# 128 bytes more between the high and the low weight buffer of a float32 transformer kernel

## What is computed

```python
h = rms_norm(x, pre_mix_norm);  p = h @ w_in            # then four mixers -> y
x = x + rms_norm(y @ w_out, post_mix_norm)
x = x + rms_norm(conv_ffn(rms_norm(x), ffn_up, ..., ffn_down), post_ffn_norm)
# second block
x = x + 0.5 * swiglu(rms_norm(x), ffn1_w_gate, ffn1_w_up, ffn1_w_down)
proj = rms_norm(x) @ w_in_2                             # then two kinds of attention
y = sigmoid(g_dil) * (o_dil @ w_dil_branch) + sigmoid(g_diff) * (o_diff @ w_diff_branch)
x = x + y @ w_out_2
x = x + 0.5 * swiglu(rms_norm(x), ffn2_w_gate, ffn2_w_up, ffn2_w_down)
```

## The kernel before, in words

| moving rows | high rows | low rows |
|---|---|---|
| moving, gated, gated_branch, branch | 192 | 192 |
| mixed (`w_out` alone) | 0 | 0 |

## Time and profile before

### The profile page before, as it was taken

One profiled execution on the slowest core, in us unless ns is written; L12 is line 12 of the kernel. 1 busy time (PEld: TensorE's weight loads), 2 busy tenths in 40 slices (PEclk: granted clock), 3 DMA queues, 4 the chain that ended last, 5 costly groups with the idle time before them and its releaser, 6 DMA issues.

```text
span 3354.0 us, 59341 instructions
## 1 busy us (share of the span) xinstructions
PE 3336.8 (99%) x19746; PEld 2930.5 (87%) x19746; DVE 2238.2 (67%) x2874; ACT 1745.4 (52%) x2588; POOL 533.8 (16%) x502
## 2 busy tenths in 40 slices
PE   9999999999999999999999999999999999999999
PEld 8888888888888888888888888888888888888888
DVE  7878587777744565655555699766687655655544
ACT  5455565555544554544444555554565554544443
POOL 0215111111100011111100066511100111111000
PEclk9999999999999999999999999999999999999999
DMA  6535555555566555555566655545556555555665
GB/s 214 163 114 157 183 171 190 189 189 191 187 193 189 179 180 194 188 188 192 188 190 191 215 175 175 190 156 160 172 192 199 192 188 192 189 188 191 186 194 174
DMA packets 176036, 616.21 MB, mean 184 GB/s; under 512 B 20912, under 2 KB 21584, under 8 KB 175568
## 3 DMA queue, kind: packets, MB, share of 16 engines
q1 hardware_dynamic: 175520, 609.84, 57.0%
q10 hardware_dynamic: 432, 5.24, 0.4%
HBM read 610.81 MB, written 4.19 MB: 183 GB/s over the span
## 4 chain that ended last, share of the span: by engine, by line
PE 94%; DVE 3%; issue 1%; ACT 1%; DMA 1%; POOL 0%; DVEq 0%; SPq 0%; ACTq 0%; POOLq 0%
PE acc L462 59%; PE acc L465 30%; DVE weights_low L312 1%; PE ps_wide L391 1%; PE acc L477 1%; ACT weights_high L305 0%; PE ps_narrow L2551 0%; PE ps_wide L2527 0%; PE acc L480 0%; DVE halves_memory L567 0%; PE ps_scale L2932 0%; DMA weights_raw<-in_w_in 0%; DMA weights_raw<-in_w_diff_branch 0%; DVE halves_memory L3010 0%; ACT arena L801 0%
## 5 line engine op out<-in xcount | busy, mean ns | idle before, releaser
L462 PE MATMUL acc<-moving_halves,weights_high 128*128 128x512 f32 x6304 | 1971.2, 394 | 1.9 <-DVE x_T L2820 1.9
L312 DVE TENSOR_TENSOR weights_low<-weights_raw,weights_high 128x1024 fp32r<-128x1024 f32 (+1 forms) x1172 | 1431.2, 1235 | 716.7 <-ACT weights_high L305 715.7
L305 ACT ACTIVATE weights_high<-weights_raw 128x1024 fp32r<-128x1024 f32 (+1 forms) x1172 | 1207.8, 1032 | 768.7 <-PE acc L465 741.9
L465 PEld LDWEIGHTS acc<-moving_halves,weights_low 128*128 128x128 f32 x6304 | 1183.8, 188 | 262.0
L465 PE MATMUL acc<-moving_halves,weights_low 128*128 128x256 f32 x6304 | 1244.8, 279 | 0.0
L462 PEld LDWEIGHTS acc<-moving_halves,weights_high 128*128 128x128 f32 x6304 | 957.5, 188 | 12.0 <-issue 9.8
L462 PE MATMUL acc<-gated_halves,weights_high 128*128 128x512 f32 x2024 | 627.9, 392 | 0.0
L561 ACT ACTIVATE cross_products<-acc 128x256 f32<-128x256 f32 x503 | 193.0, 384 | 666.3 <-PE acc L465 666.2
L465 PEld LDWEIGHTS acc<-gated_halves,weights_low 128*128 128x128 f32 x2024 | 380.1, 188 | 83.5
L584 POOL TENSOR_TENSOR stage_scratch<-unscaled,token_scale 128x256 f32<-128x256 f32 x260 | 215.0, 827 | 1279.9 <-DVE unscaled L567 802.4
L465 PE MATMUL acc<-gated_halves,weights_low 128*128 128x256 f32 x2024 | 399.3, 279 | 0.0
(11 more groups left out here) (384 smaller groups left out, 2008.7 us busy)
## 6 DMA issues: line engine op xcount, KB each, us to landing
weights_raw<-in_w_in SPq DMA_DIRECT2D x268, 512.0 KB, 3.9
weights_raw<-in_ffn_up SPq DMA_DIRECT2D x176, 512.0 KB, 4.5
weights_raw<-in_ffn_w_gate SPq DMA_DIRECT2D x176, 512.0 KB, 4.2
weights_raw<-in_ffn_w_up SPq DMA_DIRECT2D x176, 512.0 KB, 4.8
weights_raw<-in_ffn_w_down SPq DMA_DIRECT2D x160, 512.0 KB, 3.9
weights_raw<-in_ffn_down SPq DMA_DIRECT2D x80, 512.0 KB, 3.8
weights_raw<-in_w_out SPq DMA_DIRECT2D x64, 512.0 KB, 3.9
weights_raw<-in_ffn_w_down SPq DMA_DIRECT2D x32, 256.0 KB, 2.7
```

The lines of the kernel that those rows point to most:

```text
L305: core.nc.scalar.activation(core.high[:, slot, k0:nk, :].rearrange("p a b -> p (a b)"), core.raw[:, slot, k0 * P:nk * P], ACT.Copy).then_i ...
L312: core.nc.vector.tensor_tensor(core.low[:, slot, k0:nk, :].rearrange("p a b -> p (a b)"), core.raw[:, slot, k0 * P:nk * P], core.high[:, s ...
L462: core.nc.tensor.matmul(acc[:, t % 2, :, :], core.high[:, u % SLOTS, k, :], parts[:, prod.first[t] + k0 + k, :, :], start=(k0 + k == 0), s ...
L465: core.last = core.nc.tensor.matmul(acc[:, t % 2, 0, :], core.low[:, u % SLOTS, k, :], parts[:, prod.first[t] + k0 + k, 0, :], start=False ...
```

## The change

A buffer of 32 floats (128 bytes) that nothing reads or writes is allocated between `high` and `low`. `low` and all that is allocated after it lie 128 bytes further on. No instruction is added, removed or reordered. Apart from multiples of 512 bytes, the low rows then lie 320 bytes from the moving rows instead of 192, and in `w_out` 128 instead of 0; the high rows stay at 192 and 0.

```diff
@@ -161,6 +161,7 @@
         self.sb("before_weights", [P, 48], F32)
         self.raw = self.sb("weights_raw", [P, SLOTS, KG * P], F32)
         self.high = self.sb("weights_high", [P, SLOTS, KG, P], F32R)
+        self.sb("before_low", [P, 32], F32)
         self.low = self.sb("weights_low", [P, SLOTS, KG, P], F32R)
         self.cross = self.sb("cross_products", [P, 2, S], F32)
         self.z = self.sb("unscaled", [P, 2, S], F32)
```

## The result

The changed kernel takes 3394.16 us (median; 3393.37 to 3395.63) against 3356.16 before: a ratio of 1.0112, 95% interval 1.0100 to 1.0124, 38.0 us slower. The forecast was 3371, slower by 14.6 us. The direction held and the time lies in the range, but the term that carries the sum came out 2.6 times as large.

The account below looks back on a forecast made before the run. The prediction took PE's streaming pace to bound the kernel. The profiled 3355.8 us plus 14.6 for one hit more in every eight matmuls gave 3370.4, with 0.3 for the median 3370.8; range for 8 in 10: 3328 to 3400.

Parts of the forecast that it names:

- What bounds the kernel: Whole kernel: PE, busy 99% of the span and never idle in the compared windows; only its streaming pace can change the time.
- The new buffer and the shift of what lies behind `low`: Unused buffer has no instruction; moving `low` as DVE's target and later buffers by 128 bytes was taken as costing nothing.
- What acts is the low rows' distance from the moving rows: Two of four weight loads in each ordinary pair: distance 192 to 320 can change PE's pace, 44 us gain to 73 loss.
- with half of the loads moved I take half of that, one hit more: Ordinary pairs: `w_out` has two hits more in eight matmuls; half of that taken, one more, 14.6 us slower.
- the pace would be the same in all products: Sign of being right: pairs of `moving_halves` and `gated_halves` take about 0.693 us instead of 0.690 in all products.
- The hit of 6.67 ns: Each weight load beside a matmul costs PE's stream nothing or one step of 6.67 ns, above a floor of 0.680 us a pair.
- the upper bound of 73 us: Largest loss for the ordinary pairs: a hit at each of four loads, 4 instead of 1.5 a pair, 4388 x 16.7 ns.
- `w_out`: Low rows leave distance 0 while high rows stay: a gain of one hit or none, at most 0.4 us, left out.
- No change by a count of 128 bytes: Rival at each weight load: distance counts only apart from multiples of 128 bytes, time 3356; chance 0.32 for all no change.
- No change because the order of events sets the rhythm: Rival: streams settle in rhythms by event order without address changes, time 3356; chance 0.32 for all no change.
- Faster: Rival at the low loads: they lose hits, 3341, 3334, or 3312 with none left; chance 0.25.
- Much slower: Far end of the main case: all eight loads may get hits, 3400 with three more, 3429 with all; 0.07 over 3400.

Follow-up runs that it names:

- e1: Kernel before with 128 bytes added behind `low` instead of in front, so only the buffers after it move: 3356.61 us, ratio 0.9998.
- e5: Kernel before with high rows moved to distance 64 and low rows kept at 192 (apart from multiples of 256 bytes): 3368.40 us, ratio 1.0036.
- e11: Kernel before with high and low rows both put at distance 0 in all products but `w_out` (there 64): 3380.37 us, ratio 1.0072.
- e8: Changed kernel with one idle matmul ahead of each of two long streams (`ffn_up`, `ffn1` gate and up): 3375.86 us, ratio 1.0062.
- e6: Kernel before with the low rows alone moved by 64 bytes, to distance 0 with high rows at 192: 3389.86 us, ratio 1.0097.
- e10: Kernel before with the low rows alone moved by 32 bytes, to distance 224 with high rows at 192: 3431.41 us, ratio 1.0215.
- e15: Changed kernel with each 512-column high matmul made into two of 256, six matmuls and loads a pair: 3321.56 us, ratio 0.9897 to the kernel before.
- e14: Kernel before with high and low rows both at distance 64 and each 512-column high matmul made into two of 256: 3409.39 us, ratio 1.0132.

## Why the prediction was right, and where it was wrong

**What bounds the kernel: right.** PE's pace and nothing else. 36.0 of 38.2 us are found in the pairs that ran at 0.690 before, most of the rest in the other pairs, with the clock at 1.00, no idle PE in the windows and unchanged splits.

**The new buffer and the shift of what lies behind `low`, costed at nothing: right.** e1 moved the same buffers and took 3356.61 us; DVE's split went from 1235 to 1234 ns.

**What acts is the low rows' distance from the moving rows: right.** e1 rules out the buffers behind `low`, e5 the gap between high and low rows, and e11 the address by itself. 0.690 became 0.703 with no instruction changed, only an address, and the pace does not follow what the other engines do. The Trainium skill, "SBUF — State Buffer", section "Who interferes with whom", gives TensorE one read port for the moving operand and an independent one for weight loads, and has it wait for nobody; that the two are independent does not agree with 0.690 against 0.703, and a wait for another engine was not seen here either.

**The size: the step that failed is "with half of the loads moved I take half of that, one hit more".** It took the effect as a sum over loads, so that half of the loads at a new distance give half of the effect of all. The row it was scaled from was sound: e11 gives 0.697 at (0, 0) on other products. But mixtures are not means of their parts. (64, 64) costs 11 us, and (192, 64), with half of these loads, 38. In hits the forecast was four in eight matmuls, 0.6933; 2424 pairs got seven, 0.7033, and only 1122, from 2663 us on, the forecast's four. On the average it is 38.0 / 14.6 = 2.6 hits more in eight instead of one.

**That the pace would be the same in all products: wrong.** The prediction had two rhythms at one distance in the earlier trace rows and used them only for a rival without any change. They needed to stand inside the main case: a new distance may have more than one rhythm, each with its own price. With 3.3 ns for all 4388 pairs the time would have been 3371, with 13.3 for all 3414; the result lies between because the streams split up. So it is luck that the time stayed inside the range, which ends at 3400. e8 shows that the rhythm can be changed by a single matmul ahead of a stream.

**The hit of 6.67 ns: mostly right as a step of the mean, wrong as a rule for loads.** 0.680, 0.6867 and so on up, or half-way between: the long streams' mean paces lie on this grid, but for 0.698 in e6, a quarter of a step off, which is one of the prediction's own signs that the hit is not the unit. Single pairs are not on it: before the change they take 688 and 692 ns by turns, and no run shows one load that costs 6.67 ns. That a load costs at most one step is refuted by 0.713 in e10. So the upper bound of 73 us was not safe by reason. e10's slowest execution, 3439.76 us and so 83 us over the kernel before, lies beyond it.

**`w_out`: wrong in its sign, without weight.** It became slower, 0.700 instead of 0.6965, by 120 pairs x 3.5 ns = 0.4 us.

**The rivals.** *No change by a count of 128 bytes* fell: 128 bytes act, 256 and 512 don't. *No change because the order of events sets the rhythm* was half right: events choose between rhythms (the turn at 2662 us, e8), but the distance sets which there are. *Faster* did not happen in the old order; its floor of 0.680, read from the joined tiles, was reached in e15, where order and distance go together, at 3321.56 instead of the 3312 named for no hits at all. *Much slower* (three more hits, 3400) was given 0.07 over 3400; with seven hits in eight for most pairs the result came to within 6 us of it.

**What stays open.** What in the chip a hit is: the runs show a pace that depends on the addresses modulo 256 bytes (by 32 or less), on the order of loads and matmuls, and on the start of the stream. That a load and the moving rows meet in the same part of the memory is a reading of this that no run shows. Why one start gives 0.703 and another 0.693, and why (192, 192) with four loads was found in one rhythm only, is not known either; that executions of one kernel can take different rhythms is read from the spread of e8, e10 and e14, of which one execution each has a trace. A finer search for distances with six loads a pair was not tried; e15 need not be the best.

## What to carry to other kernels

Where PE is the bound and never idle, take its pace from the starts of a repeated unit in several products, and compare it with the columns at the granted clock: a gap (here 640 to 690 ns a pair, of which no ordinary stream got under 680) is time that buffers' places and the order of matmuls can change, here from 1% less to 2% more for the kernel, with no wait to show for it. Don't scale such a pace from one layout to another that mixes old and new distances; run the few layouts and orders, in pairs, since the best distance of those tried for one order, (192, 192), was a bad one for the other. If the same code shows two paces in one trace, forecast both, and look at what stands ahead of each stream.

## What the runs showed of the hardware that was not expected

- 32 bytes more ahead of one operand cost about 2% (3431.41 us, 3407 to 3440, against 3356.28; e10), while 256 and 512 bytes cost nothing.
- A stream of matmuls has rhythms, 0.6933 and 0.7033 us for the same 1536 columns at the same addresses. A rhythm lasts as long as the stream, for some 700 us here, and one idle matmul ahead of the stream replaced the one by the other (e8).
- Two matmuls of 256 columns, with a weight load each, can be faster than one of 512: 0.680 against 0.703 us a pair at (192, 64), 3321.56 against 3394.16 us in all. At (192, 192) it is the other way round, 0.707 against 0.690.
